# Value products and memory scores from operands split in two fp32r parts

## The chip, the cores and the metric

The kernel runs on one core of a Trainium2 chip. The metric is the device time of one execution in microseconds. Its engines are named as the profile names them: PE (TensorE, the matmuls) with PEld (its weight loads), DVE (VectorE), ACT (ScalarE), POOL (GpSimd) and SP (SyncE, which only issues transfers here).

## What is computed

One decoder layer on 256 tokens of width 2048, batch 1. With eight heads of differential attention, eight heads of MoBA attention (with 256 tokens there is one block, so it is plain causal attention), a SiLU gate, an output projection, and then cross-attention with four heads into a memory of 256 tokens:

```python
h = rmsnorm(x, norm_mix_g[l])
proj = jnp.einsum('bsd,de->bse', h, w_in[l])
dq, dk, dv, mq, mk, mv, gate = jnp.split(proj, SPLITS, axis=-1)
...
p = jax.nn.softmax(logits, axis=-1)
attn = p[:, :, 0] - lam.astype(jnp.float32) * p[:, :, 1]
return jnp.einsum('bhqk,bhkd->bhqd', attn.astype(v.dtype), v)
...
y = jnp.concatenate([d_out, m_out], axis=-1) * jax.nn.silu(gate)
x = x + jnp.einsum('bse,ed->bsd', y, w_out[l])
h2 = rmsnorm(x, norm_mem_g[l])
mn = rmsnorm(mem, mem_norm_g[l])
...
logits = jnp.einsum('bshd,bmhd->bhsm', q, km).astype(jnp.float32) * HEAD_DIM ** -0.5
p = jax.nn.softmax(logits, axis=-1).astype(vm.dtype)
o = jnp.einsum('bhsm,bmhd->bshd', p, vm).reshape(B, S, MEM_WIDTH)
x = x + jnp.einsum('bse,ed->bsd', o, w_o_mem[l])
```

The change concerns two of these products: the probabilities times the values (`attn` and v, and the same of MoBA), and the memory scores (q and km).

## The kernel before

**Two ways to multiply.** The large projections split each fp32 operand into a high part, rounded to the type fp32r, and a low part, the difference, also fp32r. A product is then three matmuls that add up in one PSUM bank: high by high, high by low, low by high. These are the lines 614 to 616 of `half_group`, with the weights in `w_hi` and `w_lo`. The small products (values, memory scores, memory output) are plain fp32 matmuls; the profile shows each of them as two records, so that the 6 matmuls of a pair in `attend_values` stand there as 12.

**Halves and windows.** The weights come in halves of 256 rows by 512 columns. A half is 12 matmuls on PE (two row blocks, two token tiles, three products). Two heads make a pair, and there are 8 pairs: 0 to 3 differential, 4 to 7 MoBA. A window `pair_window(j, ...)` is 16 halves, n = 0 to 15: in them PE projects queries, keys, values and gates of pair j, and between them it does the attention of pair j-1, `attend_values` behind half n = 6 (`WINDOW.values`), and the scores of pair j behind half 13. After the windows comes `TAIL`, 56 more halves (output projection, memory keys, queries and values); the last pair's values stand behind its half 5 (`LAST.values`), and the transposes of its outputs y behind half 8 (`LAST.yT_made`). Behind the first half of the memory values PE transposes the memory queries (`transpose_queries`), behind the second it makes the memory scores (`memory_scores`).

**ACT and DVE go in step with the halves.** In step n ACT first makes the high part of half n+2 (`split_hi`, line 880), DVE the low part (`split_lo`, line 1209), and only then what the step has of attention. Each has its instructions in a fixed order, and waits on semaphores. `w_hi` and `w_lo` have 4 slots, so ACT can fill a slot only when PE is done with the half four before. PE waits in each half for `lo_made`, which DVE counts up with each low part. In step 4 ACT merges the transposed probabilities of the two heads into `probT` (line 946); `v_sb` is written in steps 2 and 3 (line 938). DVE does a quarter of the SiLU in each of the steps 4 to 7 (`silu_piece`: add 1, reciprocal, multiply). In the step before `y` it computes the scale, and in step `y` (10 in a window, 8 in the tail) four products that make y; for these it waits for the SiLU and for the values.

```python
WINDOW = Slots(6, 10, None, 15)
LAST = Slots(5, 8, 8, 11)
...
for u in range(2):
    pe.wait_ge(probT_ready, 2 * a + u + 1)
    head = slice(u * P, (u + 1) * P)
    for t, i, kt in ((0, 2, 0), (1, 0, 0), (1, 1, 1)):
        m = pe.matmul(ps[:, 4 + u, t * P:(t + 1) * P], probT[:, u, i], v_sb[:, kt, head],
```

Of the kernel before, what the change touches and what calls it, by code (L numbers as in the profile page):

```python
# [22 lines left out]
F32 = mybir.dt.float32  # L23
# [80 lines left out]
QK_TURN_AT = 1  # L104
Y_TURN_AT = 6
P_TURN_AT = (10, 11)
MEM_LOAD_AT = 14


# [24 lines left out]
def program(nc, x, mem, norm_mix_g, w_in, lambda_q1, lambda_k1, lambda_q2, lambda_k2,  # L134
            subln_g, w_out, norm_mem_g, mem_norm_g, w_q_mem, w_kv_mem, w_o_mem, final_g, out):
    with ExitStack() as ctx:
# [18 lines left out]
        qT_hi = sbuf("qT_hi", [P, 2, SEQ], F32R)  # L155
        qT_lo = sbuf("qT_lo", [P, 2, SEQ], F32R)
        kT_parts = sbuf("kT_parts", [P, 2, 2, SEQ], F32R)
        v_sb = sbuf("v_sb", [P, NT, 2 * P])
        probT = sbuf("probT", [P, 2, 3, P])
        r_row = sbuf("r_row", [P, SEQ])  # L160
        ones_row = sbuf("ones_row", [1, P])
# [42 lines left out]
        qm_sb, at = carve(pool, 0, NT, COLS)  # L204
        km_sb, at = carve(pool, at, NT, COLS)
        vm_sb = qm_sb
        qmT_sb, at = carve(pool, at, 4, SEQ)
        kmT_sb, at = carve(pool, at, 4, SEQ)
        assert at <= 8 * COLS
        mem_flat = mems[:, :, :].rearrange("p t d -> p (t d)")  # L210
# [129 lines left out]
        y_merged = sem("y_merged")  # L340
        alibi_ready = sem("alibi_ready")
        gate_ready = sem("gate_ready")
        v_ready = sem("v_ready")
        silu_steps = sem("silu_steps")
        qkT_hi_ready = sem("qkT_hi_ready")
        qkT_ready = sem("qkT_ready")
# [6 lines left out]
        planes_ready = sem("planes_ready")  # L353
        planes_turned = [sem("planes_turned0"), sem("planes_turned1")]
        probT_ready = sem("probT_ready")
        pv_made = sem("pv_made")
        o_summed = sem("o_summed")
        y_steps = {"diff": sem("y_steps_diff"), "moba": sem("y_steps_moba")}
# [9 lines left out]
        q_scale_ready = sem("q_scale_ready")  # L368
        qm_ready = sem("qm_ready")
        qmT_made = sem("qmT_made")  # L370
        qmT_ready = sem("qmT_ready")
        km_ready = sem("km_ready")
        kmT_ready = sem("kmT_ready")
        vm_ready = [sem("vm_ready_dve"), sem("vm_ready_act")]
# [33 lines left out]
        out_tiles = out[0].rearrange("(t p) d -> p t d", p=P)  # L408

        kT_rows = kT_parts[:, :, :, :].rearrange("p u r s -> p (u r) s")  # L410

        def qm_rows(g, hf):

# [179 lines left out]
        def _(pe):  # L593
# [95 lines left out]
            def attend_values(n, a, slots):  # L689

                if n == slots.values:
                    pe.wait_ge(v_ready, 2 * a + 2)
                    for u in range(2):
                        pe.wait_ge(probT_ready, 2 * a + u + 1)
                        head = slice(u * P, (u + 1) * P)
                        for t, i, kt in ((0, 2, 0), (1, 0, 0), (1, 1, 1)):
                            m = pe.matmul(ps[:, 4 + u, t * P:(t + 1) * P], probT[:, u, i], v_sb[:, kt, head],  # L697
                                          start=kt == 0, stop=kt == t)
                        m.then_inc(pv_made, 1)
                if n == slots.yT_made:  # L700
                    pe.wait_ge(y_ready, a + 1)
                    for u in range(2):
                        for t in range(NT):
                            m = pe.transpose(ps[:, 6, (u * NT + t) * P:(u * NT + t + 1) * P],
                                             y_sb[:, t, u * P:(u + 1) * P], ident[:, :])
                    m.then_inc(yT_made, 1)

            def pair_window(j, kind, first=False):

                for n in range(PAIR_HALVES):  # L710
                    within = n % (2 * NG)
                    if n == 0:
                        wait(pe, qk_planes_ready, 2 * j)
                    if n == PAIR_HALVES // 2:
                        if first:
                            pe.wait_ge(gainsT_ready, 3)
                        wait(pe, v_ready, 2 * j)
                    if first and n < PAIR_HALVES // 2:
                        first_half_group(n)
                    else:  # L720
                        half_group(PAIR_HALVES * j + n, n % SPLITS, (0, 1) if n < PAIR_HALVES // 2 else (2, 3),
                                   aT_hi, aT_lo, within * (GK // 2), within == 0, within == 2 * NG - 1)
                    if first:
                        if n == 10:
                            pe.wait_ge(r_rows_ready, 1)
                            for t in range(NT):
                                m = pe.transpose(ps[:, 6, t * P:(t + 1) * P], r_rows[:, t], ident[:, :])
                            m.then_inc(r_row_made, 1)
                            pe.wait_ge(ones_ready, 1)
                            pe.wait_ge(lam_ready, 2)  # L730
                            pe.matmul(ps[:, 6, SEQ:SEQ + 1], ones_row[:, :], neg_lam_row[0:1, :], start=True, stop=True
                                      ).then_inc(lam_made, 1)
                    else:
                        attend_values(n, j - 1, WINDOW)
                    attend_scores(n, j, kind)
# [29 lines left out]

            def memory_scores():

                pe.wait_ge(qmT_ready, 2)
                pe.wait_ge(kmT_ready, 2)
                for t in range(NT):  # L770
                    for h in range(4):
                        m = pe.matmul(ps[:, (4, 0)[t] + h // 2, (h % 2) * SEQ:(h % 2 + 1) * SEQ],  # L772
                                      qmT_sb[:, h, t * P:(t + 1) * P], kmT_sb[:, h, :], start=True, stop=True)
                    m.then_inc(scores_m_made, 1)

            for w, (what, n, g) in enumerate(TAIL):
# [1 line left out]
                    pe.wait_ge(qk_planes_ready, 2 * PAIRS)  # L778
                    pe.wait_ge(yT_ready, PAIRS - 1)
                if (what, n, g) == ("out", 1, 0):  # L780
                    pe.wait_ge(v_ready, 2 * PAIRS)
                if (what, n, g) == ("out", 2, 0):
                    pe.wait_ge(x1_ready, NT * 1)
                if (what, n, g) == ("out", 3, 0):
# [84 lines left out]
        def _(act):  # L869
# [63 lines left out]
            def chunk_b_out(a, t):  # L933

                gate = ps[:, 2 + t, 2 * P:4 * P]
                act.activation(sig_sb[:, t], gate, ACT.Exp, scale=neg_r_x[:, t:t + 1])
                act.activation(gate_sb[:, t], gate, ACT.Identity, scale=r_x[:, t:t + 1]).then_inc(gate_ready, 1)
                act.activation(v_sb[:, t], ps[:, 2 + t, 0:2 * P], ACT.Identity, scale=r_x[:, t:t + 1]
                               ).then_inc(v_ready, 1)

            def merge_probabilities(a):

                for u in range(2):
# [3 lines left out]
                                   .rearrange("p (c h) -> p h c", h=2),  # L947
                                   probT_planes[:, u].rearrange("p (h c) -> p h c", h=2), ACT.Copy
                                   ).then_inc(probT_ready, 1)

            def merge_qk(a, t):

# [160 lines left out]
            for i in range(2 * len(TAIL)):  # L1113
# [26 lines left out]
                if i == 48:  # L1140
# [2 lines left out]
                    act.wait_ge(km_turned[1], 16)  # L1143
                    act.activation(qm_sb[:, 1], ps[:, 7, :], ACT.Identity, scale=q_scale[:, 1:2]
                                   ).then_inc(qm_ready, 1)
                if i == 49:
                    act.wait_ge(qmT_made, 1)
                    act.activation(qmT_sb[:, 0:2].rearrange("p h s -> p (h s)"), ps[:, 4, :], ACT.Copy
                                   ).then_inc(qmT_ready, 1)
                if i == 41:  # L1150
                    act.wait_ge(half_done, done_at("km", 0, 3))
                    act.wait_ge(r_mem_steps, 2 + RSQRT_STEPS)
# [49 lines left out]
        def _(dve):  # L1202
# [102 lines left out]
            def attend_values(n, a, kind, slots):  # L1305
# [14 lines left out]
                                                     ALU.mult, ALU.add)  # L1320
                    m.then_inc(attn_ready, 1)

                if n in (4, 5, 6, 7):
                    silu_piece(a, n - 4)
                if n == slots.chain:
                    steps = y_steps[kind.name]
                    if kind.diff:
# [138 lines left out]
            for i in range(2 * len(TAIL)):  # L1466
# [28 lines left out]
                if i == 48:  # L1495
                    dve.wait_ge(half_done, done_at("qm", 0, 3))
                    dve.tensor_scalar(qm_sb[:, 0], ps[:, 6, :], q_scale[:, 0:1], None, ALU.mult).then_inc(qm_ready, 1)
                if i == 49:
                    dve.wait_ge(qmT_made, 2)
                    dve.tensor_copy(qmT_sb[:, 2:4].rearrange("p h s -> p (h s)"), ps[:, 5, :]).then_inc(qmT_ready, 1)  # L1500
                if i == 41:
                    dve.wait_ge(half_done, done_at("km", 0, 3))
                    dve.tensor_scalar(km_sb[:, 0], ps[:, 4, :], r_mem[:, 0:1], None, ALU.mult).then_inc(km_ready, 1)
# [107 lines left out]
```

## Time and profile before

| | |
|---|---|
| time, median of 3 runs | 573.56 us (573.34 to 574.38) |
| the profiled execution: its own time | 572.92 us |
| its span, first to last instruction | 571.1 us |
| granted TensorE clock, mean | 0.996 |
| busy: PE, PEld, DVE, ACT | 562.1, 468.0, 425.9, 406.6 us |
| PE records of the pairs' values (line 697) | 96, mean 274 ns |
| PE records of the memory scores (line 772) | 16, mean 379 ns |

PE's records are longer than the distance from one to the next, because matmuls are pipelined and a record runs to the end of its own pipeline. What a matmul costs is read from the distance between starts. Where the profile groups several alike, a row gives the start of the first, the time to the end of the last, and the count.

### The profile page before, as it was taken

What the parts mean: (1) busy time and instruction counts of PE and PEld (TensorE: products, weight loads), DVE (VectorE), ACT (ScalarE), POOL (GpSimd) and SP (SyncE); (2) the same over time, 40 slices, a digit from 0 to 9 for tenths busy, and PEclk for the clock granted to TensorE, in tenths of its full rate; (3) what the DMA queues carried; (4) which work ended last, traced back from release to release, by engine and by line L of the source; (5) the groups of instructions that cost most, each with busy time, mean ns of one, the idle gap of its engine ahead of it and who ended that gap; (6) DMA issues with size and microseconds to landing.
All of it is one profiled execution on the core that took longest, in us unless ns stands there. A gap on an engine that the chain in (4) does not pass through costs nothing.

```text
span 571.1 us, 8602 instructions
## 1 busy us (share of the span) xinstructions
PE 562.1 (98%) x2640; PEld 468.0 (82%) x2640; DVE 425.9 (75%) x716; ACT 406.6 (71%) x651; POOL 2.1 (0%) x26
## 2 busy tenths in 40 slices
PE   8999999999999999999999999999999999999994
PEld 7888888888888888888888888888888888888884
DVE  4769769678886877866756768668568886877975
ACT  5786866967868778776784784875598786855543
POOL 1000000000000000000000000000000000000000
PEclk9999999999999999999999999999999999999998
DMA  8997769568676776886875976779799986983803
GB/s 272 353 280 238 210 173 250 169 201 230 190 233 192 200 216 188 234 224 163 250 215 157 264 199 192 220 194 299 246 229 266 260 248 187 260 230 111 244 2 147
DMA packets 151236, 123.32 MB, mean 216 GB/s; under 512 B 66809, under 2 KB 133162, under 8 KB 150698
## 3 DMA queue, kind: packets, MB, share of 16 engines
q1 hardware_dynamic: 151112, 122.98, 76.3%
q8 instruction: 12, 0.20, 0.1%
q14 instruction: 14, 0.11, 0.1%
q10 hardware_dynamic: 98, 0.03, 0.0%
HBM read 105.93 MB, written 2.10 MB: 189 GB/s over the span
## 4 chain that ended last, share of the span: by engine, by line
PE 98%; DVE 1%; ACT 0%; POOL 0%; issue 0%; ACTq 0%; POOLq 0%
PE ps L614 28%; PE ps L615 28%; PE ps L616 28%; PE ps L697 2%; PE ps L650 1%; PE ps L654 1%; PE ps L658 1%; PE ps L679 1%; PE ps L850 1%; PE ps L855 1%; PE ps L851 1%; PE ps L637 1%; PE ps L772 1%; PE ps L624 0%; PE ps L818 0%; PE ps L682 0%
## 5 line engine op out<-in xcount | busy, mean ns | idle before, releaser
L1209 DVE TENSOR_TENSOR w_lo<-w_raw,w_hi 128x1024 fp32r<-128x1024 f32 x183 | 222.5, 1222 | 106.2 <-ACT w_hi L880 104.2
L880 ACT ACTIVATE w_hi<-w_raw 128x1024 fp32r<-128x1024 f32 x183 | 192.6, 1057 | 82.3 <-PE ps L616 81.3
L614 PE MATMUL ps<-w_hi,aT 128*128 128x512 f32 x540 | 211.8, 392 | 0.0
L615 PE MATMUL ps<-w_lo,aT 128*128 128x512 f32 x540 | 210.3, 389 | 0.0
L616 PE MATMUL ps<-w_hi,aT 128*128 128x512 f32 x540 | 210.1, 389 | 0.0
L616 PEld LDWEIGHTS ps<-w_hi,aT 128*128 128x128 f32 x540 | 101.4, 188 | 21.2
L614 PEld LDWEIGHTS ps<-w_hi,aT 128*128 128x128 f32 x540 | 101.4, 188 | 21.0
L615 PEld LDWEIGHTS ps<-w_lo,aT 128*128 128x128 f32 x540 | 101.4, 188 | 20.4
L614 PE MATMUL ps<-w_hi,yT_hi 128*128 128x512 f32 x144 | 56.2, 390 | 0.0
L616 PE MATMUL ps<-w_hi,yT_lo 128*128 128x512 f32 x144 | 56.0, 389 | 0.0
L615 PE MATMUL ps<-w_lo,yT_hi 128*128 128x512 f32 x144 | 56.0, 389 | 0.0
L615 PEld LDWEIGHTS ps<-w_lo,yT_hi 128*128 128x128 f32 x144 | 27.0, 188 | 5.6
L614 PEld LDWEIGHTS ps<-w_hi,yT_hi 128*128 128x128 f32 x144 | 27.0, 188 | 5.6
L616 PEld LDWEIGHTS ps<-w_hi,yT_lo 128*128 128x128 f32 x144 | 27.0, 188 | 5.5
L1266 DVE RECIPROCAL pool<-pool 128x128 f32<-128x128 f32 x32 | 30.5, 953 | 1.1
L985 ACT ACTIVATE mems<-ps 128x1024 uint16<-128x1024 uint16 x16 | 15.5, 1021 | 17.0 <-PE ps L616 16.9
L1006 ACT ACTIVATE pool<-pool,small 128x256 f32<-128x256 f32 (+1 forms) x48 | 21.2, 444 | 6.9 <-DVE small L1301 6.9
L955 ACT ACTIVATE pool<-mems 128x1024 uint16<-128x1024 uint16 x16 | 21.8, 1365 | 1.1 <-DMA mems<-mems 1.1
L1293 DVE SCALAR_TENSOR_TENSOR pool<-ps,small,alibi 128x256 f32<-128x256 f32 (+2 forms) x32 | 15.0, 511 | 5.9 <-PE ps L685 5.9
L946 ACT ACTIVATE probT<-mems 128x768 uint16<-128x768 uint16 x16 | 16.0, 1077 | 0.0
L1020 ACT ACTIVATE mems<-pool 128x768 uint16<-128x768 uint16 x16 | 13.3, 832 | 2.9 <-DVE pool L1318 2.9
L885 ACT ACTIVATE aT<-ps,gainsT 128x256 fp32r<-128x256 f32 x16 | 7.5, 470 | 8.8 <-PE ps L637 8.7
(202 smaller groups left out, 569.1 us busy)
## 6 DMA issues: line engine op xcount, KB each, us to landing
w_raw<-in_w_in SPq DMA_DIRECT2D x251, 256.0 KB, 3.2
w_raw<-in_w_out SPq DMA_DIRECT2D x64, 256.0 KB, 4.0
w_raw<-in_w_kv_mem SPq DMA_DIRECT2D x32, 256.0 KB, 4.5
w_raw<-in_w_q_mem SPq DMA_DIRECT2D x16, 256.0 KB, 3.0
w_raw<-in_w_o_mem SPq DMA_DIRECT2D x16, 256.0 KB, 3.8
mems<-in_mem SPq DMA_DIRECT2D x1, 2048.0 KB, 10.1
xs<-in_x SPq DMA_DIRECT2D x3, 512.0 KB, 6.3
w_raw<-in_w_in SPq DMA_DIRECT2D x10, 128.0 KB, 5.5
```

The source lines that it names most:

```text
L614: pe.matmul(acc, hi[:, k0 + k, tok], w_hi[:, slot, k], start=first and k == 0, stop=False)
L615: pe.matmul(acc, hi[:, k0 + k, tok], w_lo[:, slot, k], start=False, stop=False)
L616: m = pe.matmul(acc, lo[:, k0 + k, tok], w_hi[:, slot, k], start=False, stop=last and k == GK // 2 - 1)
L880: act.activation(w_hi[:, i % SPLITS], raw, ACT.Copy).then_inc(hi_made, 1)
L946: act.activation(probT[:, u].rearrange("p i q -> p (i q)").bitcast(U16) .rearrange("p (c h) -> p h c", h=2), probT_planes[:, u].rearrange( ...
L955: act.activation(qkT_sb[:, :, t * P:(t + 1) * P].bitcast(U16) .rearrange("p i (q h) -> p h i q", h=2), qkT_planes[:, t].rearrange("p (h i ...
L985: act.activation(qk_planes[:, t].rearrange("p (h c) -> p h c", h=2), ps[:, t, :].bitcast(U16).rearrange("p (c h) -> p h c", h=2), ACT.Copy ...
L1006: m = act.activation(prob_sb[:, u, c, cols], prob_sb[:, u, c, cols], ACT.Exp, bias=neg_max[:, u, t, c:c + 1], accum_out=exp_sum[:, c, u, t ...
L1020: act.activation(prob_planes[:, u].rearrange("p (h c) -> p h c", h=2), prob_sb[:, u, 0, :].bitcast(U16).rearrange("p (c h) -> p h c", h=2) ...
L1209: dve.tensor_tensor(lo, w_raw[:, i % RAW], hi.bitcast(F32), ALU.subtract).then_inc(lo_made, 1)
L1266: dve.reciprocal(s, s).then_inc(silu_steps, 1)
L1293: dve.scalar_tensor_tensor(prob_sb[:, u, 0:kind.maps, cols], banks[:, :, cols], r[:, t:t + 1], bias, ALU.mult, ALU.add).then_inc(logits_re ...
```

## The change

In each pair the probabilities and the values are split as the weights are. ACT writes the values straight to fp32r (`v_hi`, line 959 of the changed file) and copies `probT` to a high part `probT_hi` (line 972); DVE makes the low parts: `v_lo` in steps 3 and 4 (one token tile each, from PSUM), `probT_lo` of both heads in step 5. A plain fp32 product becomes three fp32r ones, 18 matmuls of 128 columns in a pair. DVE's SiLU pieces go from the steps 4, 5, 6, 7 to 4, 6, 7, 8. The memory keys are split the same way in step 48 (ACT `kmT_hi`, DVE `kmT_lo`, 128x1024 each), the memory queries in step 49, and the 8 plain fp32 matmuls of the scores become 24 of 256 columns. Before, ACT and DVE copied one half of the queries each out of PSUM; now ACT copies both and DVE subtracts both. All new parts lie in buffers that are idle at the time (`cT_hi`, `cT_lo`, `kT_parts`, `qT_hi`, `qT_lo`). No transfer is added or moved. The memory output (lines 818 and 824) stays plain fp32. Declarations of semaphores are left out below.

```diff
@@ -104,6 +104,7 @@
...
 P_TURN_AT = (10, 11)
+SILU_AT = (4, 6, 7, 8)
 MEM_LOAD_AT = 14
@@ -155,7 +156,7 @@
...
         kT_parts = sbuf("kT_parts", [P, 2, 2, SEQ], F32R)
-        v_sb = sbuf("v_sb", [P, NT, 2 * P])
+        v_hi = sbuf("v_hi", [P, NT, 2 * P], F32R)
         probT = sbuf("probT", [P, 2, 3, P])
@@ -204,7 +205,7 @@
...
         vm_sb = qm_sb
-        qmT_sb, at = carve(pool, at, 4, SEQ)
+        _, at = carve(pool, at, 4, SEQ)
         kmT_sb, at = carve(pool, at, 4, SEQ)
...
@@ -408,6 +415,15 @@
...
+
+        probT_hi = cT_hi[:, 0:3].rearrange("p a s -> p (a s)").rearrange("p (u i q) -> p u i q", u=2, i=3)
+        probT_lo = cT_lo[:, 0:3].rearrange("p a s -> p (a s)").rearrange("p (u i q) -> p u i q", u=2, i=3)
+        v_lo = (cT_hi[:, 3], cT_lo[:, 3])
+
+        qmT_hi = kT_rows
+        qmT_lo = (qT_hi, qT_lo)
+        kmT_hi, kmT_lo = cT_hi, cT_lo
@@ -689,13 +705,15 @@
...
                 if n == slots.values:
-                    pe.wait_ge(v_ready, 2 * a + 2)
+                    pe.wait_ge(v_lo_ready, 2 * a + 2)
                     for u in range(2):
-                        pe.wait_ge(probT_ready, 2 * a + u + 1)
+                        pe.wait_ge(probT_lo_ready, 2 * a + u + 1)
                         head = slice(u * P, (u + 1) * P)
                         for t, i, kt in ((0, 2, 0), (1, 0, 0), (1, 1, 1)):
-                            m = pe.matmul(ps[:, 4 + u, t * P:(t + 1) * P], probT[:, u, i], v_sb[:, kt, head],
-                                          start=kt == 0, stop=kt == t)
+                            acc = ps[:, 4 + u, t * P:(t + 1) * P]
+                            pe.matmul(acc, probT_hi[:, u, i], v_hi[:, kt, head], start=kt == 0, stop=False)
+                            pe.matmul(acc, probT_hi[:, u, i], v_lo[kt][:, head], start=False, stop=False)
+                            m = pe.matmul(acc, probT_lo[:, u, i], v_hi[:, kt, head], start=False, stop=kt == t)
                         m.then_inc(pv_made, 1)
@@ -714,7 +732,7 @@
...
                             pe.wait_ge(gainsT_ready, 3)
-                        wait(pe, v_ready, 2 * j)
+                        wait(pe, v_lo_ready, 2 * j)
                     if first and n < PAIR_HALVES // 2:
@@ -765,12 +783,15 @@
...
-                pe.wait_ge(qmT_ready, 2)
-                pe.wait_ge(kmT_ready, 2)
+                pe.wait_ge(qmT_lo_ready, 2)
+                pe.wait_ge(kmT_lo_ready, 1)
                 for t in range(NT):
                     for h in range(4):
-                        m = pe.matmul(ps[:, (4, 0)[t] + h // 2, (h % 2) * SEQ:(h % 2 + 1) * SEQ],
-                                      qmT_sb[:, h, t * P:(t + 1) * P], kmT_sb[:, h, :], start=True, stop=True)
+                        acc = ps[:, (4, 0)[t] + h // 2, (h % 2) * SEQ:(h % 2 + 1) * SEQ]
+                        tok = slice(t * P, (t + 1) * P)
+                        pe.matmul(acc, qmT_hi[:, h, tok], kmT_hi[:, h], start=True, stop=False)
+                        pe.matmul(acc, qmT_hi[:, h, tok], kmT_lo[:, h], start=False, stop=False)
+                        m = pe.matmul(acc, qmT_lo[h // 2][:, h % 2, tok], kmT_hi[:, h], start=False, stop=True)
                     m.then_inc(scores_m_made, 1)
@@ -778,7 +799,7 @@
...
                 if (what, n, g) == ("out", 1, 0):
-                    pe.wait_ge(v_ready, 2 * PAIRS)
+                    pe.wait_ge(v_lo_ready, 2 * PAIRS)
                 if (what, n, g) == ("out", 2, 0):
@@ -935,8 +956,8 @@
...
                 act.activation(gate_sb[:, t], gate, ACT.Identity, scale=r_x[:, t:t + 1]).then_inc(gate_ready, 1)
-                act.activation(v_sb[:, t], ps[:, 2 + t, 0:2 * P], ACT.Identity, scale=r_x[:, t:t + 1]
-                               ).then_inc(v_ready, 1)
+                act.activation(v_hi[:, t], ps[:, 2 + t, 0:2 * P], ACT.Identity, scale=r_x[:, t:t + 1]
+                               ).then_inc(v_hi_ready, 1)
@@ -947,6 +968,8 @@
...
                                    ).then_inc(probT_ready, 1)
+                    act.wait_ge(probT_ready, 2 * a + u + 1)
+                    act.activation(probT_hi[:, u], probT[:, u], ACT.Copy).then_inc(probT_hi_ready, 1)
@@ -1143,10 +1166,13 @@
...
                                    ).then_inc(qm_ready, 1)
+                    act.wait_ge(kmT_ready, 2)
+                    act.activation(kmT_hi[:, :, :], kmT_sb[:, :, :], ACT.Copy).then_inc(kmT_hi_ready, 1)
                 if i == 49:
-                    act.wait_ge(qmT_made, 1)
-                    act.activation(qmT_sb[:, 0:2].rearrange("p h s -> p (h s)"), ps[:, 4, :], ACT.Copy
-                                   ).then_inc(qmT_ready, 1)
+                    for b in range(2):
+                        act.wait_ge(qmT_made, b + 1)
+                        act.activation(qmT_hi[:, 2 * b:2 * b + 2], ps[:, 4 + b, :].rearrange("p (h s) -> p h s", s=SEQ),
+                                       ACT.Copy).then_inc(qmT_hi_ready, 1)
                 if i == 41:
@@ -1320,8 +1346,18 @@
...
-                if n in (4, 5, 6, 7):
-                    silu_piece(a, n - 4)
+                if n in (3, 4):
+                    t = n - 3
+                    dve.wait_ge(v_hi_ready, 2 * a + t + 1)
+                    dve.scalar_tensor_tensor(v_lo[t], ps[:, 2 + t, 0:2 * P], r_x[:, t:t + 1],
+                                             v_hi[:, t].bitcast(F32), ALU.mult, ALU.subtract).then_inc(v_lo_ready, 1)
+                if n == 5:
+                    for u in range(2):
+                        dve.wait_ge(probT_hi_ready, 2 * a + u + 1)
+                        dve.tensor_tensor(probT_lo[:, u], probT[:, u], probT_hi[:, u].bitcast(F32), ALU.subtract
+                                          ).then_inc(probT_lo_ready, 1)
+                if n in SILU_AT:
+                    silu_piece(a, SILU_AT.index(n))
                 if n == slots.chain:
@@ -1495,9 +1531,15 @@
...
                     dve.tensor_scalar(qm_sb[:, 0], ps[:, 6, :], q_scale[:, 0:1], None, ALU.mult).then_inc(qm_ready, 1)
+                    dve.wait_ge(kmT_hi_ready, 1)
+                    dve.tensor_tensor(kmT_lo[:, :, :], kmT_sb[:, :, :], kmT_hi[:, :, :].bitcast(F32), ALU.subtract
+                                      ).then_inc(kmT_lo_ready, 1)
                 if i == 49:
-                    dve.wait_ge(qmT_made, 2)
-                    dve.tensor_copy(qmT_sb[:, 2:4].rearrange("p h s -> p (h s)"), ps[:, 5, :]).then_inc(qmT_ready, 1)
+                    for b in range(2):
+                        dve.wait_ge(qmT_hi_ready, b + 1)
+                        dve.tensor_tensor(qmT_lo[b][:, :, :], ps[:, 4 + b, :].rearrange("p (h s) -> p h s", s=SEQ),
+                                          qmT_hi[:, 2 * b:2 * b + 2].bitcast(F32), ALU.subtract
+                                          ).then_inc(qmT_lo_ready, 1)
                 if i == 41:
...
                     dve.tensor_scalar(km_sb[:, 0], ps[:, 4, :], r_mem[:, 0:1], None, ALU.mult).then_inc(km_ready, 1)
```

On PE, in the MoBA windows, where the values stand between two halves. Before (line 697 holds all six matmuls):

```order
L615 MATMUL ps<-w_lo,aT 128x512
L616 MATMUL ps<-w_hi,aT 128x512
L692 ISA
L694 REGISTER_ALU
L697 MATMUL ps<-v_sb,probT 128x128 x6
L131 REGISTER_ALU
L614 MATMUL ps<-w_hi,aT 128x512
```

Now, the first half of the group (`cT_hi` and `cT_lo` hold the parts of the probabilities and the low part of the values):

```order
L631 MATMUL ps<-w_lo,aT 128x512
L632 MATMUL ps<-w_hi,aT 128x512
L708 ISA
L710 REGISTER_ALU
L714 MATMUL ps<-v_hi,cT_hi 128x128
L715 MATMUL ps<-cT_hi 128x128
L716 MATMUL ps<-v_hi,cT_lo 128x128
L714 MATMUL ps<-v_hi,cT_hi 128x128
L715 MATMUL ps<-cT_hi 128x128
L716 MATMUL ps<-v_hi,cT_lo 128x128
```

The three rows come six times in a pair in place of the one row of six.

On DVE, in the tail, steps 5 to 8, where the last pair is finished. Before:

```order
L1209 TENSOR_TENSOR w_lo<-w_raw,w_hi 128x1024 [waits hi_made]
L1264 TENSOR_SCALAR pool<-pool 128x128 [waits gate_ready]
L1266 RECIPROCAL pool<-pool 128x128 [waits silu_steps]
L1268 TENSOR_TENSOR pool<-pool 128x128 [waits silu_steps]
L1346 RECIPROCAL small<-small 128x4
L1209 TENSOR_TENSOR w_lo<-w_raw,w_hi 128x1024 [waits hi_made,y_steps_moba]
L1354 SCALAR_TENSOR_TENSOR pool<-ps,small,pool 128x128 [waits silu_steps,pv_made]
L1354 SCALAR_TENSOR_TENSOR pool<-ps,small,pool 128x128 x3
```

Now:

```order
L1235 TENSOR_TENSOR w_lo<-w_raw,w_hi 128x1024 [waits hi_made]
L1357 TENSOR_TENSOR cT_lo<-probT,cT_hi 128x384 [waits probT_hi_ready] x2
...
L1382 RECIPROCAL small<-small 128x4
L1235 TENSOR_TENSOR w_lo<-w_raw,w_hi 128x1024 [waits hi_made,y_steps_moba]
L1290 TENSOR_SCALAR pool<-pool 128x128 [waits gate_ready]
L1292 RECIPROCAL pool<-pool 128x128 [waits silu_steps]
L1294 TENSOR_TENSOR pool<-pool 128x128 [waits silu_steps]
L1390 SCALAR_TENSOR_TENSOR pool<-ps,small,pool 128x128 [waits silu_steps,pv_made]
L1390 SCALAR_TENSOR_TENSOR pool<-ps,small,pool 128x128 x3
```

The two subtractions for the probabilities stand in step 5, and the last SiLU piece stands right ahead of the four products of y.

## Rows read from the trace of the kernel before

**Rows 1.** The page: busy us (share) xinstructions, and the granted clock in 40 slices.
```profile
PE 562.1 (98%) x2640; PEld 468.0 (82%) x2640; DVE 425.9 (75%) x716; ACT 406.6 (71%) x651; POOL 2.1 (0%) x26
PEclk9999999999999999999999999999999999999998
```

**Rows 2.** The page: share of each engine in the chain that ended last.
```profile
PE 98%; DVE 1%; ACT 0%; POOL 0%; issue 0%; ACTq 0%; POOLq 0%
```

**Rows 3.** Timeline of PE inside one half: start us, us, engine, what.
```profile
330.09 0.39 PE L614 MATMUL ps<-w_hi,aT 128*128 128x512 f32 x1
...
333.49 0.39 PE L614 MATMUL ps<-w_hi,aT 128*128 128x512 f32 x1
```

**Rows 4.** Timeline of PE around the values of a MoBA pair.
```profile
260.38 1.50 PE L697 MATMUL ps<-v_sb,probT 128*128 128x128 f32 x12
...
262.42 0.39 PE L614 MATMUL ps<-w_hi,aT 128*128 128x512 f32 x1
```

**Rows 5.** Timeline of PE at the end, pieces of 256 columns, fp32r.
```profile
560.86 0.28 PE L850 MATMUL ps<-w_hi,cT_hi 128*128 128x256 f32 x1
...
562.29 0.28 PE L850 MATMUL ps<-w_hi,cT_hi 128*128 128x256 f32 x1
```

**Rows 6.** Timeline of PE around the scores of a MoBA pair, fp32r.
```profile
234.70 0.40 PE L679 MATMUL ps<-kT_parts,qT_hi 128*128 128x256 f32 x2
...
235.77 0.22 PE L685 MATMUL ps<-kT_parts,qT_lo 128*128 128x128 f32 x1
235.83 0.45 PE L614 MATMUL ps<-w_hi,aT 128*128 128x512 f32 x1
...
236.57 0.40 PE L614 MATMUL ps<-w_hi,aT 128*128 128x512 f32 x1
```

**Rows 7.** Timeline of PE around the memory scores, plain fp32.
```profile
518.28 3.61 PE L772 MATMUL ps<-pool 128*128 128x256 f32 x16
...
522.42 0.39 PE L614 MATMUL ps<-w_hi,aT 128*128 128x512 f32 x1
```

**Rows 8.** Groups by line and shape: busy us, mean ns of one | idle before, releaser.
```profile
L1214 DVE SCALAR_TENSOR_TENSOR aT<-ps,gainsT,aT 128x256 fp32r<-128x256 f32 x16 | 7.7, 481 | 6.7 <-ACT aT L885 6.7
L1281 DVE TENSOR_TENSOR qT_lo<-pool,qT_hi 128x512 fp32r<-128x512 f32 x8 | 5.5, 683 | 0.0
L994 ACT ACTIVATE qT_hi<-pool 128x512 fp32r<-128x512 f32 x8 | 4.9, 616 | 0.0
```

**Rows 9.** Timeline of DVE in a MoBA window, its first work behind step 8.
```profile
267.57 1.23 DVE L1209 TENSOR_TENSOR w_lo<-w_raw,w_hi 128x1024 fp32r<-128x1024 f32 x1 [4.68 <-ACT w_hi L880]
```

**Rows 10.** Timelines of the last pair in the tail: ACT, DVE, PE.
```profile
388.95 1.97 ACT L946 ACTIVATE probT<-mems 128x768 uint16<-128x768 uint16 x2
```
```profile
391.85 1.22 DVE L1209 TENSOR_TENSOR w_lo<-w_raw,w_hi 128x1024 fp32r<-128x1024 f32 x1
...
398.37 0.22 DVE L1264 TENSOR_SCALAR pool<-pool 128x128 f32<-128x128 f32 x1
...
399.83 0.17 DVE L1346 RECIPROCAL small<-small 128x4 f32<-128x4 f32 x1
401.38 1.23 DVE L1209 TENSOR_TENSOR w_lo<-w_raw,w_hi 128x1024 fp32r<-128x1024 f32 x1 [1.38 <-ACT w_hi L880]
402.52 1.12 DVE L1354 SCALAR_TENSOR_TENSOR pool<-ps,small,pool 128x128 f32<-128x128 f32 x4
```
```profile
395.88 1.50 PE L697 MATMUL ps<-v_sb,probT 128*128 128x128 f32 x12
...
405.40 0.60 PE L704 MATMUL ps<-ident,pool 128*128 128x128 f32 x4
```

**Rows 11.** Timelines of ACT and DVE ahead of the memory scores.
```profile
512.73 1.05 ACT L880 ACTIVATE w_hi<-w_raw 128x1024 fp32r<-128x1024 f32 x1
515.30 0.60 ACT L1148 ACTIVATE pool<-ps 128x512 f32<-128x512 f32 x1 [1.52 <-PE ps L761]
```
```profile
513.81 1.22 DVE L1209 TENSOR_TENSOR w_lo<-w_raw,w_hi 128x1024 fp32r<-128x1024 f32 x1 [0.92 <-ACT w_hi L880]
```

More of the change, by code:

```diff
@@ L342, in program @@
         gate_ready = sem("gate_ready")
-        v_ready = sem("v_ready")
+        v_hi_ready = sem("v_hi_ready")
+        v_lo_ready = sem("v_lo_ready")
         silu_steps = sem("silu_steps")
@@ L355, in program @@
         probT_ready = sem("probT_ready")
+        probT_hi_ready = sem("probT_hi_ready")
+        probT_lo_ready = sem("probT_lo_ready")
         pv_made = sem("pv_made")
@@ L370, in program @@
         qmT_made = sem("qmT_made")
-        qmT_ready = sem("qmT_ready")
+        qmT_hi_ready = sem("qmT_hi_ready")
+        qmT_lo_ready = sem("qmT_lo_ready")
+        kmT_hi_ready = sem("kmT_hi_ready")
+        kmT_lo_ready = sem("kmT_lo_ready")
         km_ready = sem("km_ready")
```

## Prediction

> **What bounds the kernel now.** First the page. PE is busy 98% of the span at a granted clock of 1.0 in all slices but the last [rows 1], and the chain that ended last is PE by 98% [rows 2]. So I ask of each part how long PE is occupied by it, and only then whether ACT and DVE (71% and 75% busy) still deliver ahead of PE. I cost PE by distances between starts in its timeline, since its records overlap.
>
> The unit is the fp32r matmul of 512 columns: from 330.09 to 333.49 there are 15 distances, 3.40 us, so 0.2267 us each [rows 3].
>
> **The values, before.** The group of one pair begins at 260.38. The first matmul of the half behind it is stretched, so I measure to the fourth, at 262.42, and take off three units: 2.04 - 0.68 = 1.36 us for 12 records [rows 4], 0.113 each. Eight pairs: 10.9 us.
>
> **The values, now.** 18 fp32r matmuls of 128 columns. No such run stands in the trace, so I bound its pace from two rows.
> - From above: fp32r matmuls of 256 columns, 12 distances from 560.86 to 562.29, 0.119 us each [rows 5].
> - From below: 512 columns take 0.227 and 256 take 0.119, so on that line 256 columns are worth 0.108, and 128 columns would take 0.119 - 0.054 = 0.065 us.
> - Between the ends a row decides. The scores of a MoBA pair are ten fp32r matmuls, eight of 256 columns and two of 128. From 234.70 to the fourth large matmul behind them, 236.57, less three units, is 1.87 - 0.68 = 1.19 us [rows 6]. The eight take 0.95, and 0.24 is left for two: 0.12 each, as much as 256 columns. The recorded start of the next matmul, 0.06 behind the 128-column one (235.77, 235.83), says otherwise, but that next matmul is itself stretched, so the time is only booked later.
>
> My reading is that each fp32r matmul brings a weight load of 128 columns, and the load of the next can't begin before the present matmul has taken its own; with 256 columns streaming and loading are equal, with 128 the load is longer. Every matmul has its own load, 2640 of each [rows 1], so two neighbours with the same stationary operand save nothing. The Trainium skill, "TensorE: Matmul & The Clock Gate", section "LDWEIGHTS (loading the stationary operand)", gives a load as its column count over 1.2, which for 128 is an estimate of 107 ns; the trace's 0.119 is near it. By that page's pace the sum would be a little under mine and of the same sign.
>
> So 18 x 0.119 = 2.14 us a pair, +0.78 against 1.36, and for eight pairs **+6.3 us**. Ends: 18 x 0.065 = 1.17, -0.19 a pair, -1.5 us in all; and 18 x 0.12 = 2.16, +6.4. I take the upper, since the score group is the nearest row. A middle value worth naming is the pace of the plain records themselves, 0.113, which have a load each as well: 2.03, +0.67 a pair, +5.4.
>
> **The memory scores.** Before: 518.28 to 522.42 less three units, 4.14 - 0.68 = 3.46 us [rows 7]. Now 24 x 0.119 = 2.86 [rows 5]. **-0.6 us**. This group gains and the other loses by one mechanism: a plain product of 256 columns takes two records of 0.216, three fp32r ones take 0.36; of 128 columns it takes 0.226, and the three still 0.36.
>
> **ACT and DVE in the windows.** Per pair ACT gets two copies of 128x384, at most 0.62 each (128x512 takes 0.616), and waits for its own merge before each, which undoes an overlap of some 0.1: at most 1.4 us. DVE gets two low parts of values at 0.48 and two of probabilities at 0.68 at most: 2.3 us [rows 8]. The ready-made cover is the long idle behind step 8, 4.68 us in a MoBA window [rows 9]; there the SiLU piece that moves to step 8 ends. Costed at nothing, and looked at where it is tightest, in the last pair, whose values come one half (2.72 us) earlier than in a window:
> - ACT's merges begin at 388.95. With the copies the next high part, and so DVE's low part of step 5, slips from 391.85 to at most 393.3, ends at 394.5, and the two subtractions end at 395.2 and 395.9. PE wants the first at 395.88, the second nine matmuls (1.07 us) later [rows 10]. Cover of 0.7 us.
> - In step 8 DVE's low part starts when PE frees a slot, 401.38 plus the 0.8 that PE is now later. Then 1.14 for it, 1.46 for the SiLU piece (398.37 to 399.83) and 1.12 for the products of y: 405.9. PE's transposes come at 405.40 + 0.8 = 406.2 [rows 10]. Cover 0.3 us, the thinnest; if it is gone, PE waits by what is missing, once.
> - In a window the same order has 2.7 us more ahead of the values, and y is made in step 10, not 8.
>
> Behind DVE's added waits (for ACT's copies, in steps 3 to 5) its low parts of the weights queue; PE is two halves, 5.4 us, from needing them. SP gets nothing; its loads follow `lo_made` eight halves ahead.
>
> **ACT and DVE ahead of the memory scores.** ACT's copy of the keys takes some 1.05 and moves its split from 512.73 to 513.7. DVE subtracts the keys from 513.8 to 515.0, makes its low part until 516.2 (it began at 513.81), and after ACT's two copies (515.30 to 516.5) the two subtractions of 0.68 end at 517.6. PE is there at 518.28 [rows 8, 11]. Cover 0.7 us, cost nothing. DVE's next low part then is half a microsecond late with PE three halves away.
>
> **Sum.** +6.3 - 0.6 = +5.7 us. The profiled execution took 572.92 us, 1.8 more than its span of 571.1 and 0.6 under the median of 573.56. It would become 578.6, with a span of 576.8; against the median **579.2 us**, +1.0%.
>
> **Rivals.**
> - **A. Columns set the pace.** A 128-column fp32r matmul costs 0.065, for instance because the 0.24 us in the score group is a cost of changing shapes and not of loads. Then -1.5 - 0.6 = -2.1 us: 571.5, faster. For it: the recorded 0.06. Against: the plain values, measured across the same two changes of shape, come out at 0.113 a record, little over half of the 0.216 of a plain record of 256 columns [rows 4, 7], so changing shapes costs less than 0.1 us in all there. The same would follow from the Trainium skill, "FP8 and Floating Point Precision", section "TensorE Precision Notes": true fp32 is four passes through the array, so three replace four.
> - **B. A pace between.** Loads overlap better in a long run of small matmuls than in the pair of neighbours seen, and one costs about 0.08, a third of the way from 0.065 to 0.119. Then 18 x 0.08 = 1.44, +0.08 a pair, +0.6 - 0.6 = 0: 573.6, no change. The Trainium skill, "TensorE: Matmul & The Clock Gate", section "Back-to-back issue gap", has such a pace, about 81 ns at 128 columns with loads. No run of fp32r matmuls here shows it, and rows 6 speak against it.
> - **C. ACT and DVE become late.** If the narrow copies and subtractions cost as much as 1024 columns (1.05 and 1.22 in the rows of the weights [rows 9, 11]) the low probabilities come some 2 us later than above, and PE waits 1.3 us in the last pair and up to 1 us in each window. It decides when the first `probT_lo` ends past PE's arrival at the values. Price 1 to 5 us on top: 580.5 to 584.
> - That the change does not do what it says (the products staying plain) is excluded by the order on PE, three matmuls on `v_hi`, `cT_hi`, `cT_lo` in place of one on `probT`.
>
> **Chances.** The forecast 0.82 (its own range 578.0 to 580.4, from 0.113 to 0.12 and half a microsecond of waits); A 0.05; B 0.05; C 0.08. With 577.5 to 582.0 the range holds the forecast and most of C, and leaves out A and B. About 0.2% (1.1 us) is what a measurement can tell from no change: faster 0.05, same 0.05, slower 0.90.
>
> **What would show it.** In the profile after: the 144 records of the values stand about 0.12 us apart, and the distance from one pair's group to the next grows by 0.78 us. If they stand 0.06 to 0.08 apart, A or B holds. The memory scores take 2.9 us instead of 3.46. PE shows no idle time before the values, before the transposes of y in the tail, or before the memory scores; if it does, C. DVE's idle behind step 8 shrinks from 4.7 by about 2 us. The clock stays at 1.0. The forecast would be wrong most of all if one row, the score group, misled me on the pace.

## Result and profile after

The changed kernel takes 578.48 us, median of 4 runs (578.03 to 580.29), against 573.45 us for the kernel before, run beside it. The ratio is 1.0088, with a 95% interval of 1.0068 to 1.0108. It is slower by 5.0 us; 579.2 was forecast, with 577.5 to 582.0 as the range.

The page of the changed kernel, the lines that answer to [rows 1, 2]:

```profile
span 578.5 us, 8766 instructions
PE 569.0 (98%) x2696; PEld 474.7 (82%) x2696; DVE 440.5 (76%) x750; ACT 417.3 (72%) x669; POOL 2.1 (0%) x26
PEclk9999999999999999999999999999999999999998
PE 97%; DMA 1%; DVE 1%; ACT 0%; ACTq 0%; issue 0%; SPq 0%
```

56 matmuls and 56 weight loads more, PE still at 98%. This profiled execution is the slowest of the four (580.29 us), and 2.25 us of its span are lost before the first scores begin. The chains that ended last show it: start us, us, what. The first scores, in the kernel before and in the changed one:

```profile
49.05 0.55 PE ps L679 x6
```

```profile
51.30 0.55 PE ps L695 x6
```

From there to the end it is 571.1 - 49.05 = 522.05 us before and 578.5 - 51.30 = 527.20 after, 5.15 more, which agrees with the 5.0 us of the medians within their interval (3.9 to 6.2 us). I return to the start at the end.

**The value products.** The timeline of PE in the changed kernel, around the values of a MoBA pair, answers to [rows 4]:

```profile
265.45 0.22 PE L714 MATMUL ps<-v_hi,cT_hi 128*128 128x128 f32 x1
265.51 0.28 PE L715 MATMUL ps<-cT_hi 128*128 128x128 f32 x1
265.62 0.27 PE L716 MATMUL ps<-v_hi,cT_lo 128*128 128x128 f32 x1
265.74 0.27 PE L714 MATMUL ps<-v_hi,cT_hi 128*128 128x128 f32 x1
...
267.30 0.28 PE L716 MATMUL ps<-v_hi,cT_lo 128*128 128x128 f32 x1
267.41 0.44 PE L630 MATMUL ps<-w_hi,aT 128*128 128x512 f32 x1
...
268.16 0.40 PE L630 MATMUL ps<-w_hi,aT 128*128 128x512 f32 x1
```

From the second record (265.51) to the last of the 18 (267.30) there are 16 distances in 1.79 us: 0.112 us each. Only the first distance is recorded as 0.06; its missing half stands in the stretched large matmul behind the group, as it did in [rows 6]. By the method of [rows 4] the group takes 268.16 - 265.45 - 0.68 = 2.03 us against 1.36. The distance between windows, which holds everything, is the better ruler. In the chain of the changed kernel the scores of three MoBA pairs begin at

```profile
286.72 0.35 PE ps L695 x3
...
333.50 0.35 PE ps L695 x3
...
380.28 0.35 PE ps L695 x3
```

so a window is 46.78 us. Before, it is 46.07:

```profile
234.87 0.35 PE ps L679 x3
...
280.94 0.35 PE ps L679 x3
```

That is +0.71 us, and for eight pairs +5.7. By two_products below, 0.66 of it comes with the six more matmuls and 0.05 with the type.

**The memory scores.** The timeline of PE, answering to [rows 7]:

```profile
526.20 0.28 PE L792 MATMUL ps<-cT_hi,kT_parts 128*128 128x256 f32 x1
...
528.95 0.28 PE L794 MATMUL ps<-cT_hi,qT_lo 128*128 128x256 f32 x1
529.07 0.40 PE L630 MATMUL ps<-w_hi,aT 128*128 128x512 f32 x1
...
529.76 0.40 PE L630 MATMUL ps<-w_hi,aT 128*128 128x512 f32 x1
```

24 matmuls in 2.87 us, 0.120 each, in place of 3.46: -0.6 us. Together +5.7 - 0.6 = +5.1 us, against 5.15 from the first scores on and 5.0 by the medians.

**ACT and DVE.** Of PE's waits in the changed kernel (line waited for: us in total, times, longest) only the start and one row of the new work are new or changed:

```profile
PE ps L666 <- ACT w_hi L918: 0.5, 1, 0.5
PEld ps L722 <- DVE pool L1390: 0.2, 1, 0.2
```

The second is the weight load of the transposes of y in the tail, where the forecast saw its thinnest cover. The timelines of DVE and PE there, answering to [rows 10]:

```profile
402.35 1.22 DVE L1235 TENSOR_TENSOR w_lo<-w_raw,w_hi 128x1024 fp32r<-128x1024 f32 x1
...
409.28 1.23 DVE L1235 TENSOR_TENSOR w_lo<-w_raw,w_hi 128x1024 fp32r<-128x1024 f32 x1 [1.58 <-ACT w_hi L901]
410.42 0.22 DVE L1290 TENSOR_SCALAR pool<-pool 128x128 f32<-128x128 f32 x1
...
412.06 1.13 DVE L1390 SCALAR_TENSOR_TENSOR pool<-ps,small,pool 128x128 f32<-128x128 f32 x4
```

```profile
413.07 0.39 PE L632 MATMUL ps<-w_hi,yT_lo 128*128 128x512 f32 x1
413.30 0.60 PE L722 MATMUL ps<-ident,pool 128*128 128x128 f32 x4
```

The products of y end at 413.19, and the transposes start at 413.30, 0.23 us behind the large matmul ahead of them, as in undisturbed running. The 0.3 us of cover had 0.1 left. No time was lost: from the transposes to the fourth large matmul behind their start it is 1.13 us, and it was 1.12 before. Only the weight load ahead of them started later, 0.06 us before its matmul.

### The profile page after: what moved, and what is told of

The parts are those of the page before. It is cut to its first block, busy times and chain, and to the rows that moved or that the text cites. A ratio compares the mean times of both kernels' runs of the same rounds, so it can differ in the third digit from the quotient of the medians.

```text
span 578.5 us, 8766 instructions
## 1 busy us (share of the span) xinstructions
PE 569.0 (98%) x2696; PEld 474.7 (82%) x2696; DVE 440.5 (76%) x750; ACT 417.3 (72%) x669; POOL 2.1 (0%) x26
## 4 chain that ended last, share of the span: by engine, by line
PE 97%; DMA 1%; DVE 1%; ACT 0%; ACTq 0%; issue 0%; SPq 0%
PE ps L630 28%; PE ps L631 28%; PE ps L632 27%; PE ps L666 1%; PE ps L670 1%; PE ps L674 1%; PE ps L695 1%; PE ps L871 1%; PE ps L876 1%; PE ps L872 1%; PE ps L716 1%; PE ps L715 1%; PE ps L714 1%; DMA w_raw<-in_w_in 1%; PE ps L653 1%; PE ps L839 0%
## 5 line engine op out<-in xcount | busy, mean ns | idle before, releaser
L967 ACT ACTIVATE probT<-mems 128x768 uint16<-128x768 uint16 x16 | 17.2, 1075 | 0.0
```

What stands on the lines that cost most here:

```text
L967: act.activation(probT[:, u].rearrange("p i q -> p (i q)").bitcast(U16) .rearrange("p (c h) -> p h c", h=2), probT_planes[:, u].rearrange( ...
```

## Experiments

Each kernel starts from the changed kernel or from the one before, as said. All times are against the kernel before run on the same chip (573.12 us in the first group, 573.35 in the second). As single executions of one kernel spread by about 2 us (572.70 to 574.93 for the kernel before, in the first group), the distance between MoBA windows in the trace ("windows" below) is given beside them; within a trace it repeats to 0.01 us.

### memory_only: the kernel before, memory scores alone split

> The kernel before with the memory scores alone split. Theory (PE is the bound and pays by the matmul's pace): 24 fp32r matmuls of 256 columns at 0.119 us in place of 3.46 us, so 0.6 us less than before, about 572.9 us, faster than both kernels; PE has no idle time ahead of the scores. Rival (the keys' and queries' parts come late, or the softmax chain behind the scores is the bound there): no change, 573.4 or more.

572.90 us, ratio 0.9990 (0.9980 to 1.0000); windows 46.07 us. The scores stand 0.120 us apart, PE has no idle time ahead of them. From the first scores (49.13) to the end of its span (570.7) it is 521.57 us, 0.5 less than before. The gain is where it was expected and of its size, but the times alone hardly tell it from none: 0.1% faster than the kernel before, with an interval from 0.2% to nothing. Of the kernels that compute everything it has the lowest median.

### values_only: the kernel before, value products alone split

> The kernel before with the value products alone split. Theory: 0.70 us more in each of eight pairs, as the distance between windows grew in the changed kernel (46.08 to 46.78), so 573.5 + 5.6 = 579.1 us, and values_only less memory_only is the sum of both effects. Rival (the two parts cost or gain something through each other): another difference than 5.6 us from before.

579.94 us, ratio 1.0108 (1.0090 to 1.0126), 0.8 us over the expectation. Its windows are those of the changed kernel (46.78 us). From the first scores, 50.35, to the end, 578.2, it is 527.85 us, 5.8 more than before and 0.65 more than the changed kernel, the missing gain of the memory scores. So the two parts add up: 5.8 - 0.5 = 5.3 us, against 5.15 in the changed kernel. The medians of values_only and memory_only are 7.0 us apart, where 6.2 was expected. From the first scores on it is 6.28; the rest lies ahead of them, where the two profiles differ by 1.2 us (50.35 and 49.13).

### parts_plain: all parts made, plain products

```diff
-                            pe.matmul(acc, probT_hi[:, u, i], v_hi[:, kt, head], start=kt == 0, stop=False)
-                            pe.matmul(acc, probT_hi[:, u, i], v_lo[kt][:, head], start=False, stop=False)
-                            m = pe.matmul(acc, probT_lo[:, u, i], v_hi[:, kt, head], start=False, stop=kt == t)
+                            m = pe.matmul(acc, probT[:, u, i], v_hi[:, kt, head].bitcast(F32),
+                                          start=kt == 0, stop=kt == t)
```

> The changed kernel with all parts made by ACT and DVE and waited for by PE, but the value products plain fp32 again (probabilities whole, values the high part alone, so the low part of the values is left out of the result). Theory (the added work of ACT and DVE is wholly covered, the loss is PE's alone): the loss goes away, 573.5 - 0.6 = 572.9 us, windows of MoBA 46.07 us apart. Rival C (ACT and DVE late): some of the 5.6 us stays, 574 us or more.

573.23 us, ratio 0.9998 (0.9986 to 1.0010). MoBA scores begin at 280.67 and 326.75, 46.08 us apart. Its page:

```profile
span 570.3 us, 8670 instructions
PE 561.3 (98%) x2648; PEld 467.7 (82%) x2648; DVE 440.4 (77%) x750; ACT 417.1 (73%) x669; POOL 2.1 (0%) x26
```

ACT and DVE do all the work of the changed kernel, and the 5.7 us of the values are gone. The median does not show the 0.6 us of the memory scores, but from the first scores (48.78) to the end of the span it is 521.52 us, as in memory_only (521.57), which makes no parts of the values. So the 14.5 us of added work on DVE and 10.5 on ACT cost nothing. Rival C falls.

### silu_back: the SiLU pieces in their old steps

```diff
-SILU_AT = (4, 6, 7, 8)
+SILU_AT = (4, 5, 6, 7)
```

> The changed kernel with the SiLU pieces back in steps 4 to 7. Theory: nothing changes, 578.3 us, since DVE has cover in either order; in the tail the products of y end some 1.4 us earlier and the low probabilities are not later than before, as they stand ahead of the piece in step 5. Rival (the order was needed): DVE's low weights or the low probabilities come late, PE idles, 579 us or more. A loss of 0.1 us ahead of the transposes of y, if there was one, would go.

578.52 us, ratio 1.0090 (1.0073 to 1.0107), the changed kernel's time. From the first scores (49.59) to the end of its span (576.8): 527.2 us, the same. The products of y now start at 408.71 in the tail, long before they are wanted, and PE's wait for them is gone from its list. The move of the pieces is worth nothing and costs nothing.

### cols64 and cols256: the moving operand

```diff
-                            acc = ps[:, 4 + u, t * P:(t + 1) * P]
+                            acc = ps[:, 4 + u, t * P:t * P + 64]
+                            head = slice(u * P, u * P + 64)
```

> The changed kernel with 64 moving columns instead of 128 in the value products; half of each head's values is left out. Theory (the weight load of 128 columns sets the pace below 256 columns): the matmuls stay 0.112 us apart, MoBA windows 46.8 us. Rival A or B (moving columns have a share in it): about 0.03 us less for each, windows 46.3 us or less.

```diff
-                            acc = ps[:, 4 + u, t * P:(t + 1) * P]
-                            pe.matmul(acc, probT_hi[:, u, i], v_hi[:, kt, head], start=kt == 0, stop=False)
+                            acc = ps[:, 4 + u, t * P:(t + 2) * P]
+                            pe.matmul(acc, probT_hi[:, u, i], v_hi[:, kt], start=kt == 0, stop=False)
```

The other two products take `v_lo[kt]` and `v_hi[:, kt]` in the same way.

> The changed kernel with 256 moving columns in the value products (both heads' values each time, so that the products of the second head go to wrong places). Theory: twice the columns cost only 0.007 us a matmul, 0.119 against 0.112, 0.13 us a window: 46.9 us. Rival (pace goes with columns): 0.05 us more for each, windows 47.7 us.

One run each: 578.34 and 579.29 us, windows 46.77 and 46.90 us. A pair's values in the timeline of cols64, and of cols256:

```profile
263.70 0.28 PE L717 MATMUL ps<-v_hi,cT_lo 128*128 128x64 f32 x1
...
265.37 0.28 PE L717 MATMUL ps<-v_hi,cT_lo 128*128 128x64 f32 x1
```

```profile
263.99 0.28 PE L714 MATMUL ps<-v_hi,cT_hi 128*128 128x256 f32 x1
...
266.03 0.28 PE L716 MATMUL ps<-v_hi,cT_lo 128*128 128x256 f32 x1
```

15 distances in 1.67 us are 0.111 each, 17 in 2.04 are 0.120. Half the columns save nothing, twice the columns cost 0.008 a matmul. At 128 moving columns the streaming isn't what is paid for; rivals A and B fall.

### stat64: the stationary operand

```diff
-                            acc = ps[:, 4 + u, t * P:(t + 1) * P]
-                            pe.matmul(acc, probT_hi[:, u, i], v_hi[:, kt, head], start=kt == 0, stop=False)
+                            acc = ps[0:64, 4 + u, t * P:(t + 1) * P]
+                            pe.matmul(acc, probT_hi[:, u, i, 0:64], v_hi[:, kt, head], start=kt == 0, stop=False)
```

> The changed kernel with 64 stationary columns (half of the queries of each tile; the other half is left out) and 128 moving columns. Theory (it is the load, and the load goes by its columns): the pace falls to that of the 128 moving columns, 0.06 to 0.07 us, windows 46.0 us, the values near 1.2 us. Rival (a fixed cost of any fp32r matmul, whatever is loaded): still 0.112 us apart, windows 46.8 us.

The other two products take 64 columns of `probT_hi` and `probT_lo` in the same way. 571.66 us in its one run. Matmuls and weight loads of a pair's values in its timelines:

```profile
260.47 0.22 PE L714 MATMUL ps<-v_hi,cT_hi 128*64 128x128 f32 x1
260.53 0.22 PE L715 MATMUL ps<-cT_hi 128*64 128x128 f32 x1
...
261.49 0.22 PE L716 MATMUL ps<-v_hi,cT_lo 128*64 128x128 f32 x1
```

```profile
260.53 0.14 PEld L716 LDWEIGHTS ps<-v_hi,cT_lo 128*64 128x64 f32 x1
260.59 0.13 PEld L714 LDWEIGHTS ps<-v_hi,cT_hi 128*64 128x64 f32 x1
```

Weight loads of the changed kernel, for comparison, and the scores of two MoBA pairs in the chain of stat64:

```profile
265.57 0.19 PEld L716 LDWEIGHTS ps<-v_hi,cT_lo 128*128 128x128 f32 x1
265.68 0.19 PEld L714 LDWEIGHTS ps<-v_hi,cT_hi 128*128 128x128 f32 x1
```

```profile
280.82 0.35 PE ps L695 x3
...
326.69 0.35 PE ps L695 x3
```

17 distances in 1.02 us: 0.060 us each, and windows of 45.87 us. The loads, 0.11 us apart with 128 columns, are 0.06 apart with 64. The same number of matmuls with the same moving columns go almost twice as fast when half as many stationary columns are loaded, and the group takes about 0.9 us less. So there is no fixed cost of 0.112 for a matmul; what is paid for goes with the width of the stationary operand, and the records of the load shrink with it (0.19 us to 0.14). Two things are left open. The 0.060 is only an upper bound for a load of 64 columns, as 128 moving columns might take as long (the prediction's line gave 0.065). And the edit also halves the rows of PSUM that a matmul writes, which no run separates from the load.

### two_products: as many matmuls as the plain product has records

```diff
-                            pe.matmul(acc, probT_hi[:, u, i], v_lo[kt][:, head], start=False, stop=False)
```

> The changed kernel without high probabilities by low values: 12 fp32r matmuls a pair in place of the 12 records of plain fp32 (a third of the split product is left out). Theory (a matmul costs its load, plain or fp32r): the pair costs what it did before, windows 46.1 us, whole time 573.5 - 0.6 = 572.9 us. Rival: by columns streamed it would be far cheaper, 12 x 0.065 = 0.8 us, windows 45.5 us and 568.5 us.

572.88 us, ratio 0.9988 (0.9977 to 0.9999), windows 46.12 us. Twelve fp32r matmuls cost a pair 0.05 us more than the twelve plain records did. So at 128 columns the type has almost no price: an fp32r matmul costs what a record of the plain product does. That the plain record is bound by its load too, as the expectation has it, is not shown. Plain records of 256 columns take 0.216 us, and half of that, 0.108, is my estimate of a plain record of 128 columns by its streaming alone, too near to 0.113 to tell; no run narrows the plain product. The time equals that of memory_only, but with a product left out.

### fused_loads: as many columns, fewer loads

```diff
-                            acc = ps[:, 4 + u, t * P:(t + 1) * P]
-                            pe.matmul(acc, probT_hi[:, u, i], v_hi[:, kt, head], start=kt == 0, stop=False)
-                            pe.matmul(acc, probT_hi[:, u, i], v_lo[kt][:, head], start=False, stop=False)
-                            m = pe.matmul(acc, probT_lo[:, u, i], v_hi[:, kt, head], start=False, stop=kt == t)
+                            acc = ps[:, 4 + u, t * 2 * P:(t + 1) * 2 * P]
+                            pe.matmul(acc, probT_hi[:, u, i], v_parts[:, kt, :, head], start=kt == 0, stop=False)
+                            m = pe.matmul(acc[:, 0:P], probT_lo[:, u, i], v_hi[:, kt, head], start=False, stop=kt == t)
```

The parts of the values now lie side by side in `kT_parts` (`v_parts`), and ACT's and DVE's readers of the product take the first 128 columns of each result.

> The changed kernel with the high and the low part of the values side by side, so that one matmul of 256 moving columns serves both products of a high probability: 12 matmuls and 12 weight loads a pair in place of 18, with as many columns streamed (18 x 128). The second product lands in columns of its own and is not added up, so the low part of the values is left out of the result. Theory (a matmul costs the larger of its load and its columns, 0.112 or 0.119 us): 6 x 0.119 + 6 x 0.112 = 1.39 us in place of 2.01, MoBA windows 46.2 us, whole time near 573.2 us. Rival (columns streamed set the time): nothing changes, 46.8 us and 578.3 us.

573.73 us in its one run, beside 573.70 for the kernel before; windows 46.14 us. It streams all 2304 columns of a pair (18 x 128) and takes as long as two_products with 1536 (12 x 128), since both have twelve loads:

```profile
282.10 0.35 PE ps L696 x3
...
328.24 0.35 PE ps L696 x3
```

```profile
282.34 0.35 PE ps L695 x3
...
328.46 0.35 PE ps L695 x3
```

The first two rows are the scores of two MoBA pairs in the chain of fused_loads (46.14 us), the other two those of two_products (46.12). The sum of the two parts, two additions of 128x256 a pair on DVE, was not built. Even if they cost PE nothing, which no run shows, the window of 46.14 would match that of the plain product (46.07), not beat it.

## Why the prediction was right

**The bound.** PE alone, by 98%, with everything else hidden: parts_plain and silu_back show it.

**The pace, the step on which all rested.** I chose the upper of two bounds for a 128-column fp32r matmul (0.065 to 0.12) because of one row, the score group, and gave the weight load as the reason. The pace is 0.112, and the reason bears out as far as the runs go: cols64 excludes the moving columns, stat64 ties the pace to the stationary ones, and fused_loads counts by loads. The term was a little too large. I took 0.119, the pace at 256 columns, for 128 columns too, which makes +6.3 us; it came to +5.7. The middle value, that of the plain records (0.113), was the right pace and would have given +5.4. Nor are streaming and loading equal at 256 columns, as I had it: with the same loads cols256 goes at 0.120 and the changed kernel at 0.112. So 0.12 is no load pace; that it is the pace of the columns fits the 0.227 at 512, but no run with 256 moving columns and a narrower load tests it. With the values 0.6 us too high the sum was 5.7 where 5.15 came, and the forecast of 579.2 lay 0.7 us over the median.

**The memory scores.** -0.6 us forecast, 3.46 to 2.87 us in the trace.

**The covers.** The thinnest was put at 0.3 us and had 0.1 left. I had counted the last SiLU piece as 1.46 us, to the start of an instruction that does not wait for it; the products of y do wait for it, and they start 1.64 us after the piece does (410.42 to 412.06). The copies and subtractions of 128x384 took 0.53 and 0.55 us, where at most 0.62 and 0.68 were allowed:

```profile
L972 ACT ACTIVATE cT_hi<-probT 128x384 fp32r<-128x384 f32 x16 | 8.4, 526 | 0.5
L1357 DVE TENSOR_TENSOR cT_lo<-probT,cT_hi 128x384 fp32r<-128x384 f32 x16 | 8.2, 552 | 0.0
```

DVE's idle time behind step 8 of a MoBA window went from 4.68 to 3.55 us; I had said it would shrink by about 2, and it shrank by 1.1.

**The rivals.** A and B needed a pace that goes with the moving columns, which cols64 and cols256 exclude at 128 columns. The Trainium skill, "TensorE: Matmul & The Clock Gate", has both rules that were weighed. "LDWEIGHTS (loading the stationary operand)", time by the columns loaded, agrees with stat64 (0.112 to 0.060 us for half the columns), where 0.060 is an upper bound. The 81 ns of "Back-to-back issue gap" for 128 moving columns appears in no fp32r run here with 128 stationary columns: it is 0.112 us.

## What to carry to other kernels

Splitting a plain fp32 product in three fp32r ones pays by the moving columns: with 128 stationary columns each matmul costs at least its weight load, 0.112 us here, so at 128 moving columns the product goes from two records (0.23 us) to three (0.34), and at 256 from 0.43 to 0.36. At 128 moving columns or fewer, count the loads before and after, not the columns. If a product must be split there, the parts of the moving operand can be laid side by side, so that one load serves both; fused_loads shows what that saves on PE, but not what the missing sum of the parts costs. And when one row of a trace decides between two bounds, measure it across the change of shape to steady running, since the records at the edge put the time in the wrong place.

## What I had not expected

The start of the kernel moves by 2.25 us between these profiles, far more than the 0.6 us of the memory scores. The first scores begin at 49.05 us in the profile of before, at 49.13 in memory_only, 49.59 in silu_back, 50.22 in two_products, 50.35 in values_only and 51.30 in the changed kernel, though the change touches no instruction ahead of them. In the changed kernel's profile PE waits 0.53 us for the first high part of the weights, and then its large matmuls stand about 0.43 us apart until about 11.5 us, where before they stand 0.23 apart from the second pair on:

```profile
6.05 1.19 PE L666 MATMUL ps<-w_hi,aT 128*128 128x512 f32 x2 [0.53 <-ACT w_hi L918]
7.04 1.06 PE L670 MATMUL ps<-w_hi,aT 128*128 128x512 f32 x2
7.89 1.06 PE L674 MATMUL ps<-w_lo,aT 128*128 128x512 f32 x2
```

Such a slow stretch is no mark of the changed kernel. The kernel before has its first two large matmuls about 0.46 apart. In silu_back, two_products and values_only, PE stays slow until about 8.2, 9.4 and 9.7 us, and the later it ends, the later the first scores begin. The profile's granted clock is 1.00 in that stretch all the same, so I can't say that it was the clock, although 512 columns in 0.43 us is what its lower level of 1.2 GHz would give. The cause stays open. For a comparison within 0.2% it means that the span from a fixed point behind the start, or the distance between windows, says more than a median of a few runs.
